# Norms computed by chunks of 128 channels in a two-layer decoder trunk on one core

## The reference

```
cond = silu(c)
for l in range(2):
    sh1, sc1, g1, sh2, sc2, g2 = split(cond @ ada_w[l] + ada_b[l], 6)
    h = rmsnorm(x, norm1_g[l]) * (1 + sc1) + sh1
    x = x + g1 * token_mixer(h, ...)      # w_in: 52 blocks of 128 columns, w_out: 8
    h = rmsnorm(x, norm2_g[l]) * (1 + sc2) + sh2
    x = x + g2 * peer(h, ...)             # wq: 16 blocks, u: 128 blocks, v: 128 blocks
return rmsnorm(x, final_g)
```

## Time and profile before

| | us |
|---|---|
| median of 3 runs | 2356.86 (2356.41 to 2359.24) |
| profiled execution | 2359.32 |
| its span | 2357.5 |
| TensorE busy | 2187.6 (93%) |
| VectorE busy | 1669.8 (71%) |
| ScalarE busy | 1168.8 (50%) |
| GpSimd busy | 399.3 (17%) |
| DMA, mean over the span | 174 GB/s |

### The profile page before, as it was taken

How to read it: one execution, slowest core, us unless ns; L and a number is a source line. 1 busy time by engine, 2 the same in 40 slices (tenths; PEclk the granted TensorE clock), 3 DMA queues, 4 the chain that set the end, 5 groups by cost and what they waited for, 6 DMA issues and landing times.

```text
span 2357.5 us, 42432 instructions
## 1 busy us (share of the span) xinstructions
PE 2187.6 (93%) x14848; PEld 2009.6 (85%) x14848; DVE 1669.8 (71%) x2958; ACT 1168.8 (50%) x1990; POOL 399.3 (17%) x324
## 2 busy tenths in 40 slices
PE   1999979999999999999969996999999999999996
PEld 1988969999999978888868896999999998888885
DVE  7877546999777678887654666399996776666665
ACT  2336535544666544544534373454456565544543
POOL 0000000000499800000000000000009994000000
PEclk7999989999999999999979998999999999999998
DMA  7764534555433378887533333455553333555552
GB/s 270 271 220 157 168 106 154 186 179 186 144 115 110 118 255 288 292 291 242 192 121 118 122 121 134 143 179 184 181 170 125 112 113 133 190 193 195 189 194 89
DMA packets 111570, 409.77 MB, mean 174 GB/s; under 512 B 12384, under 2 KB 12896, under 8 KB 110688
## 3 DMA queue, kind: packets, MB, share of 16 engines
q1 hardware_dynamic: 111456, 408.24, 51.0%
HBM read 406.62 MB, written 1.57 MB: 173 GB/s over the span
## 4 chain that ended last, share of the span: by engine, by line
PE 75%; POOL 16%; DVE 5%; ACT 2%; issue 1%; DMA 1%; SPq 0%; ACTq 0%; DVEq 0%
PE ps L1273 30%; POOL hot L363 16%; PE ps L1015 13%; PE ps L1019 12%; PE ps L1016 12%; PE ps L1196 1%; PE ps L1127 1%; PE ps L1037 1%; DVE big L604 1%; PE ps L1227 1%; PE ps L1053 1%; DMA raw<-in_win 1%; DVE w_lo L599 1%; ACT w_hi L377 1%; DVE big L654 1%
## 5 line engine op out<-in xcount | busy, mean ns | idle before, releaser
L599 DVE TENSOR_TENSOR w_lo<-raw,w_hi 128x1024 fp32r<-128x1024 f32 x664 | 814.3, 1227 | 343.6 <-ACT w_hi L377 321.6
L377 ACT CAST w_hi<-raw 128x1024 fp32r<-128x1024 f32 x664 | 694.9, 1047 | 706.9 <-PE ps L1019 648.8
L1015 PE MATMUL ps<-h_hi,w_hi 128*128 128x256 f32 x3136 | 791.2, 290 | 63.9 <-DVE h_lo L668 63.7
L1016 PE MATMUL ps<-h_lo,w_hi 128*128 128x256 f32 x3136 | 774.9, 284 | 0.0
L1015 PEld LDWEIGHTS ps<-h_hi,w_hi 128*128 128x128 f32 x3136 | 606.1, 193 | 79.0 <-DVE h_lo L668 65.3
L363 POOL TENSOR_SCALAR hot<-con,rt 128x128 f32<-128x128 f32 x320 | 399.1, 1261 | 1569.5 <-DVE neg L952 1569.5
L1016 PEld LDWEIGHTS ps<-h_lo,w_hi 128*128 128x128 f32 x3136 | 606.7, 193 | 0.9 <-issue 0.5
L1019 PE MATMUL ps<-h_hi,w_lo 128*128 128x256 f32 x3136 | 442.3, 284 | 0.4 <-DVE w_lo L599 0.4
L1019 PEld LDWEIGHTS ps<-h_hi,w_lo 128*128 128x128 f32 x3136 | 406.8, 193 | 0.8 <-DVE w_lo L599 0.8
L1273 PE MATMUL ps<-w_hi,p_hi 128*128 128x512 f32 x1024 | 275.3, 391 | 5.0 <-ACT p_hi L567 5.0
L567 ACT CAST p_hi<-big 128x256 fp32r (+1 forms) x256 | 103.8, 406 | 350.4 <-PE ps L1273 349.3
(11 more groups left out here) (172 smaller groups left out, 1512.7 us busy)
## 6 DMA issues: line engine op xcount, KB each, us to landing
raw<-in_u SPq DMA_DIRECT2D x256, 512.0 KB, 3.5
raw<-in_v SPq DMA_DIRECT2D x256, 512.0 KB, 3.5
raw<-in_win SPq DMA_DIRECT2D x104, 512.0 KB, 3.7
hot<-in_ada SPq DMA_DIRECT2D x80, 512.0 KB, 3.6
raw<-in_wq SPq DMA_DIRECT2D x32, 512.0 KB, 3.5
big<-in_ada SPq DMA_DIRECT2D x16, 512.0 KB, 8.5
raw<-in_wout SPq DMA_DIRECT2D x16, 512.0 KB, 3.6
big<-in_decay SPq DMA_DIRECT2D x2, 1536.0 KB, 9.2
```

What stands on the lines that cost most here:

```text
L377: nc.scalar.copy(w_hi[:, j % 2, :], raw[:, j, :]).then_inc(hi_ready, 1)
L599: tt(w_lo[:, j % 2, :], raw[:, j, :], w_hi[:, j % 2, :].bitcast(F32), ALU.subtract).then_inc(lo_ready, 1)
L1015: mm(o, w, h_hi[:, k, :], start=(k == 0), stop=False)
L1016: mm(o, w, h_lo[:, k, :], start=False, stop=False)
```

## The change

Norms work by chunks. Scaling, biased rounding and rest are done per chunk, with one `low` in the middle. The first two blocks of the stage after a norm are done together, chunk by chunk (`project_pair`). The last expert block closes bank after bank, so that the copies can start; turning, update, square and sum are interleaved. The prologue has 16 slots for `ada` rows in four groups, each loaded without waits, with two weight blocks behind each of the first two; VectorE reduces a group just ahead of the two chunks that need it. The output is written in four parts.

```diff
 SyncE, prologue
+            sp.dma_start(rs[:, 0, :].bitcast(I32), positions.partition_broadcast(P)).then_inc(pos_in, 16)
             sp.dma_start(con[:], consts).then_inc(small_in, 16)
-            sp.dma_start(vec[:], vectors).then_inc(small_in, 16)
             sp.dma_start(cond[:], c.partition_broadcast(P)).then_inc(c_in, 16)
-            sp.dma_start(rs[:, 0, :].bitcast(I32), positions.partition_broadcast(P)).then_inc(pos_in, 16)
             sp.dma_start(xT[:], x).then_inc(x_in, 16)
-            for n in range(MOD_SLOTS):
-                mod_load(0, n, mod_ring0, mod_in0, n, 0)
-            for j in range(RING):
-                load(lambda l, m: win[l, m], 0, j, 0, 0)
-            for n in range(MOD_SLOTS, MOD_FIRST):
-                mod_load(0, n, mod_ring0, mod_in0, n % MOD_SLOTS, n - MOD_SLOTS + 1)
+            sp.dma_start(vec[:], vectors).then_inc(vec_in, 16)
+            for g in range(MOD_FIRST // MOD_GROUP):
+                for j, n in enumerate((SH1 + 2 * g, SH1 + 2 * g + 1, SC1 + 2 * g, SC1 + 2 * g + 1)):
+                    sp.dma_start(mod_first[:, MOD_GROUP * g + j, :], ada[0, n]).then_inc(mod_in0[g], 16)
+                if g < RING // 2:
+                    for j in (2 * g, 2 * g + 1):
+                        load(lambda l, m: win[l, m], 0, j, 0, 0)
...
-            sp.wait_ge(result, 1)
-            sp.dma_start(out, hf).then_inc(stored, 16)
-            sp.wait_ge(stored, 16)
+            for k in range(0, KC, 2):
+                sp.wait_ge(result, k + 2)
+                sp.dma_start(out[:, k:k + 2, :], hf[:, k:k + 2, :]).then_inc(stored, 16)
+            sp.wait_ge(stored, 16 * (KC // 2))
 ScalarE (norm before: lines 406 to 420)
-            round_hi(1, 1)
+            def squares(q):
+                nc.scalar.activation(small[:, 0, 3, 0:1], eps, ACT.Abs_reciprocal_sqrt)
+                for k in range(KC):
+                    if q == 0:
+                        if k == 0:
+                            act.wait_ge(x_in, 16)
+                            act.wait_ge(cond_ready, 1)
+                    else:
+                        act.wait_ge(x_ready, KC * (q - 1) + k + 1)
+                    nc.scalar.activation(sq[:, k, :], xT[:, k, :], ACT.Square).then_inc(sq_ready, 1)
+            def root(q):
+                act.wait_ge(ssq_ready, q + 1)
+                nc.scalar.activation(rs[:, 0, :], bank(E[1])[:, 0:SEQ], ACT.Abs_reciprocal_sqrt, bias=eps,
+                                     scale=1.0 / D).then_inc(root_ready, 1)
+            def norm(q, sh, n):
+                l = q // 2
+                squares(q)
+                round_hi(n + 1, (n + 1) % RING)
+                root(q)
+                for k in range(KC):
+                    act.wait_ge(scaled_x, KC * q + k + 1)
+                    nc.scalar.activation(h_hi[:, k, :], hf[:, k, :], ACT.Identity, bias=mod[:, l, sh + k:sh + k + 1]
+                                         ).then_inc(hhi_ready, 1)
...
                 for g in range(4):
-                    act.wait_ge(y_done, l + 1)
-                    nc.scalar.copy(words(W_PJ, 4, 512)[:, g, :], bank(Y[g])).then_inc(y_copied, 1)
+                    if g < 3:
+                        act.wait_ge(y_done, 3 * l + g + 1)
+                    else:
+                        act.wait_ge(block_done, (l + 1) * N_BLOCKS)
+                    nc.scalar.copy(words(W_PJ, 4, 512)[:, g, :], bank(Y[2 * (g % 2) + g // 2])).then_inc(y_copied, 1)
+            squares(2 * DEPTH)
+            root(2 * DEPTH)
 VectorE (norm before: lines 640 to 668)
+            def rstd_chain(q):
+                ssq = bank(E[1])[:, 0:SEQ]
+                dve.wait_ge(root_ready, q + 1)
+                st.link(tt(ysq, y0, y0, ALU.mult))
+                st.link(stt(ysq, ssq, D * EPS, ysq, ALU.add, ALU.mult))
+                st.link(stt(rstd, ysq, -3.0 * D, y0, ALU.add, ALU.mult))
+            def scale(k):
+                return stt(hf[:, k, :], xT[:, k, :], alpha[:, k:k + 1], rstd, ALU.mult, ALU.mult)
+            def h_low(q, sh, k):
+                dve.wait_ge(hhi_ready, KC * q + k + 1)
+                stt(h_lo[:, k, :], hf[:, k, :], mod[:, q // 2, sh + k:sh + k + 1], h_hi[:, k, :].bitcast(F32),
+                    ALU.add, ALU.subtract).then_inc(h_ready, 1)
+            def norm(q, gain, sc, sh, n):
+                l = q // 2
+                if q:
+                    gains(l, gain, sc, 0, KC)
+                    rstd_chain(q)
                 for k in range(KC):
+                    if q == 0 and k % 2 == 0:
+                        g = k // 2
+                        dve.wait_ge(mod_in0[g], 16 * MOD_GROUP)
...                     four tensor_tensor_reduce, bias, gains of chunks 2g and 2g + 1
+                        if g == 0:
+                            rstd_chain(q)
+                            dve.wait_ge(trig_made, 1)
+                            low(0, 0)
+                    scale(k).then_inc(scaled_x, 1)
+                    if k:
+                        h_low(q, sh, k - 1)
+                    if k == LOW_AT:
+                        low(n + 1, (n + 1) % RING)
+                h_low(q, sh, KC - 1)
...
-                for k in range(N_WOUT):
+                for k in range(N_WOUT - 1):
                     low(l * N_BLOCKS + B_WOUT + k + 1, (k + 1) % RING)
...
                     stt(xT[:, k, :], bank(4 + k // 2)[:, SEQ * (k % 2):SEQ * (k % 2 + 1)],
-                        mod[:, l, G1 + k:G1 + k + 1], xT[:, k, :], ALU.mult, ALU.add).then_inc(out_taken, 1)
-                dve.wait_ge(out_taken, l * EV + B_WQ)
-                nc.vector.tensor_copy(small[:, 0, 0, 0:1], small[:, 0, 0, 0:1]).then_inc(x_ready, 1)
-                norm(2 * l + 1, V_N2 + KC * l, SC2, SH2)
+                        mod[:, l, G1 + k:G1 + k + 1], xT[:, k, :], ALU.mult, ALU.add).then_inc(x_ready, 1)
+                low(l * N_BLOCKS + B_WQ, B_WQ % RING)
+                norm(2 * l + 1, V_N2 + KC * l, SC2, SH2, l * N_BLOCKS + B_WQ)
 TensorE
+            def project_pair(q, n, e):
...                 with_hi: hi by hi, with_lo: h_lo by w_hi, low_with_hi: h_hi by w_lo; s is the block's slot
+                pe.wait_ge(hi_ready, n + 2)
+                ge(pe, out_taken, e)
+                pe.wait_ge(lo_ready, n + 1)
+                for k in range(KC):
+                    pe.wait_ge(hhi_ready, KC * q + k + 1)
+                    for s in range(2):
+                        with_hi(s, k)
+                    low_with_hi(0, k)
+                    if k:
+                        pe.wait_ge(h_ready, KC * q + k)
+                        for s in range(2):
+                            with_lo(s, k - 1)
+                pe.wait_ge(h_ready, KC * (q + 1))
+                with_lo(0, KC - 1).then_inc(block_done, 1)
+                pe.wait_ge(lo_ready, n + 2)
+                for k in range(KC):
+                    low_with_hi(1, k)
+                with_lo(1, KC - 1).then_inc(block_done, 1)
...
+                for f in range(2):
+                    for t in range(TB):
+                        for which in range(3):
+                            last = part(1, t, f, which, False, which == 2)
+                        if f and t:
+                            last.then_inc(block_done, 1)
+                        else:
+                            last.then_inc(y_done, 1)
+                q = 2 * l + 2
+                for k in range(KC + 2):
+                    if k < KC:
+                        pe.wait_ge(y_copied, 4 * l + (4 if k >= KC // 2 else 2))
+                        if k >= 2:
+                            pe.wait_ge(x_ready, KC * (q - 1) + k - 1)
+                        for t in range(TB):
+                            src = words(W_PJ, 4, 512)[:, 2 * (k // 4) + t, P * (k % 4):P * (k % 4 + 1)]
+                            last = turn(bank(M[k % 2])[:, P * t:P * (t + 1)], src, ident)
+                        last.then_inc(y_turned, 1)
                     if k >= 2:
+                        square_sum(q, k - 2)
```

More of the change, by code:

```diff
@@ L576, in outputs @@
                             round_p(m + 2, j % 2)
[L577 removed]
+                        if not (end and (j == 3 or j == 2 and l == DEPTH - 1)):
                             round_hi(n + 2, (j + 2) % RING)
@@ L670, in stage @@
-            def stage(l, base, count, extra=None, per=0, last_one=True):
-                n0 = l * N_BLOCKS + base
-                def body(i):
-                    for j in range(RING):
-                        low(n0 + RING * i + j + 1, (j + 1) % RING)
-                        if extra is not None:
-                            extra(i, j)
-                st.loop(count // RING, per, body)
+            dve.wait_ge(sig_c, 1)
+            tt(cond[:], cond[:], words(W_SQ, D), ALU.mult).then_inc(cond_ready, 1)
@@ L1029, in stage @@
                 if count > ahead:
                     with pe.Fori(0, count // LONG) as i:
-                        body(i, ahead, LONG)
-            def norm(q):
-                for k in range(KC):
```

(44 more changed lines are left out.)

178 lines of the change are left out of this document (76 added, 102 removed).

## The result

The kernel after takes 2291.92 us (median of 4 runs, 2291.22 to 2293.4), the kernel before 2357.01 beside it (4 runs, 2356.41 to 2359.24): ratio 0.9723, 95% interval 0.9706 to 0.974. The forecast was 2294.0, range 2284 to 2311.

What follows compares the result with a forecast made beforehand. TensorE, 93% busy, was taken as bound, idle mainly in five norms. Savings of 8.0 + 15.4 + 14.5 + 15.4 + 9.7 = 63 us from the 2356.86 median gave 2293.9, range 2284 to 2311.

Steps and rivals of the forecast that it cites:

- Norms 1 and 3: Output projection to query projection: second block done at 312.0 instead of 327.4, 15.4 us saved in each, 30.8 together.
- Block 2 needs ScalarE's rounding: hidden: After the pair in norms 1 and 3: rounding starts at 310.2, ends at 311.3, before the second block is done at 312.0.
- The reason given for the early squares: Before norms 1 and 3: with `low` behind the `xT` updates, these follow the banks as they close, ending near 297.2.
- Norm 2: End of layer 0: sums end at 1190, second block done at 1202.0 instead of 1216.6, 14.5 us saved, between 11 and 17.
- Norm 4: End of the kernel: sums end at 2340.3, span at 2347.8 instead of 2357.5, 9.7 us saved, between 6 and 12.
- Norm 0: Prologue: first weight block at 17.9, root at 27.4, second block done at 56.0 instead of 65.2; 8.0 us saved, 5 to 11.
- the 1.2 for block 2: After the prologue's pair: 1.2 us added for block 2 at half clock, since TensorE's dense work begins only at the tail.
- Signs of being wrong: VectorE chunk steps over 1.0 apart, clock at half through a pair, or a block after the pair waiting for weights.
- Half clock: Rival, 20% with partial cases: TensorE stays at 1.2 GHz through sums and pair, costing 17 us in all: 2311.
- Warm throughout: Rival, 14%: full clock and all covers hold, giving 2287 us.
- Functions apart: Rival, 13%: square or biased copy shares no table with the new root, two more 1.28 us loads per norm: 2303.
- Serial chunks: Rival, 3% together with no gain: queue order makes each chunk wait for the one before, norms slower than before: 2392.

Runs made afterwards that it cites:

- The old chain: Kernel after, but with `Sqrt`, a reciprocal and six linked VectorE operations for the root in each norm, as before: 2304.48 us, ratio 0.9774.
- the serial order: Kernel after, but with each chunk's `h_low` directly behind its scaling, so VectorE waits for ScalarE's rounding every chunk: 2313.17 us, ratio 0.9814.
- the single blocks: Kernel after, but with the first two blocks after a norm done one after the other, only the first by chunks: 2305.66 us, ratio 0.9781.
- the other order of the prologue: Kernel after, but ScalarE squares x before rounding weight blocks 0 and 1, and VectorE makes block 0's `low` before the chain: 2288.51 us, ratio 0.9709.

## Why the prediction was right

**Norms 1 and 3** (15.4 each, measured 14.9 and 14.8). The parts came out as worked: sums at 0.46 a chunk for 0.43, clock 1.00 in the sums, three linked operations, 8.1 from first scaling to last `h_low`. From the end of the sums to the end of the pair are 11.7, forecast 12.0. Missed: the step "Block 2 needs ScalarE's rounding: hidden". The rounding was hidden; the `take` of the bank, in ScalarE's queue behind another rounding, was not, and cost 0.45. The reason given for the early squares, the place of `low`, is worth only 0.3. The old chain costs 2.6 in a norm, the serial order 5.6, 0.9 of it by the half clock behind the last chunk, the single blocks about 4.

**Norm 2** (14.5, measured 16.6). Copies, load and first square came as forecast, TensorE stood 1.2 for the square. Mis-sized was the clock: I took 1190 for the end of the sums, between 1188.0 and 1193.3; counted from the end of the copies it came at 1187.5. The turn of a chunk takes 0.22 at full clock, not 0.43: the four in 1.11 of the earlier trace rows are two chunks, and they ran at the half clock, to which it had fallen at 1181.5; the 0.76 of the earlier trace rows is the mean of the microsecond of the fall. The forecast's full-clock case so had the half clock's price for every turn. The clock fell later, during the pair (the stretch of 1167 to 1168), and cost nothing there: from the end of the sums to the pair's end are 11.7 here and 11.7 in norm 1, because VectorE sets the pace of the pair. Norm 3 shows the same, with the clock at half from 1412.2 to 1415.6 in its pair and a stretch as long as norm 1's.

**Norm 4** (9.7, measured 11.3). The same choice between the clocks: sums at full pace. The end of the output behind the last scaling was 2.5, forecast 2.3.

**Norm 0** (8.0, measured 9.5). The first block was there at 15.9, not 17.9, and the root was done at 25.1, not 27.4. I had taken before's landing time less four rows at the steady rate of the earlier trace rows; the queue reached over 400 GB/s sooner in the new order, from 4.5 on and not from 9, with small transfers ahead. VectorE without a break from the chain on was right. So was the half clock of the pair; but the 1.2 for block 2 was not needed, the clock being 1.00 from 54 on, while 0.6 went to later waits for weight blocks: the lead over before falls from 10.1 at 57 to 9.5 at 84.

**Sum.** 68.1 by the spans against 63: norm 0 gave 1.5 more, norm 2 2.1, norm 4 1.6, the varying expert stage 0.9, and norms 1 and 3 1.1 less. By the medians it is 65.1, and the forecast is 2.1 too high. Part of this closeness is luck: the sum was 5.1 short by the spans, and 3.0 of that were made up by how the two profiled executions lay to their medians. The forecast is carried by norms 1 and 3, whose steps held; norms 0, 2 and 4 each missed by 1.5 to 2.1, all to the same side.

**Signs of being wrong.** Two of the three appeared, and neither meant what the prediction made of it. The clock stayed at half through the pair of norm 0 (29.8 to 53.7), where the sum itself had it so and VectorE set the pace; and the blocks behind that pair waited for their weights, for 0.6 in all. VectorE's chunk steps were 0.80, and once in each pair 1.9, around `low`.

**Rivals.** *Half clock* does not hold in the sums of norms 1 to 4; in the pairs of norms 0, 2 and 3 the clock did fall, in norms 2 and 3 with no price. It has one in three of the experiments: 2 a norm with single blocks, 1.7 around norm 2 when the banks close together, 0.9 a norm in series. *Warm throughout* is nearest to what happened in norms 2 and 4. *Functions apart* falls: one table load a norm. *Serial chunks* would have needed 7 a norm; the serial order itself costs 5.0 to 5.8 and still leaves the kernel 43.5 faster than before.

A rule weighed before was the drain with each switch of tables in the Trainium skill (ScalarE: Activation LUTs, What ACT_TABLE_LOAD costs), by which 1.38 more would come with each. No run shows it: the load starts 0.01 to 0.02 after the instruction ahead of it in norms 1 and 2, the one behind it starts 0.01 to 0.02 after its 1.28, and taking the loads off the path gave 5.1 by the medians and 3.8 by the spans, not the 7 that load and drain together would have made.

## What to carry to other kernels

Where several engines hand over a tensor, the gain from chunks comes from the order within each queue: keep one chunk's work of the same engine between producing and needing a result (5.0 to 5.8 a norm here), and give TensorE a second block so that it stays fed (4 a norm). Then read each engine's queue for work that stands in front of the critical one and doesn't need to: a table load, a rounding and two `low` were worth another 9.5 by the medians. Take both clocks as ends of a range, and ask first whether TensorE sets the pace in that stretch at all.

## What was not expected of the hardware

- TensorE's first work ran in part at the half clock's pace, and the clock column doesn't say so. The sixteen products of the prologue's sums are 0.43 apart up to 22.9 and 0.22 apart from then on; they took 5.70, and 6.59 with the other order of the prologue, which starts them 2.0 earlier, where 3.69 is the full clock's time in norm 1 and 6.44 the half clock's. The trace's records of the clock begin at 23.0 (22.8 with the other order), and ahead of them the column reads 1.00.
- The same code falls to the lower clock in one place and not in another: turns and sums of norm 2 at 1.28 a chunk with the banks closed together, norm 4 of the same kernel at 0.65. What decides was not settled. Stretches at the half clock also come and go in work without an edit, as in the last experts, at 1.4 to 1.7 each.
- The biased rounding, `Square`, `Copy` and the inverse root run without a further table load once the inverse root's table is there.
